# Attention as two sequences over a whole layer, outputs three tiles behind the logits, and the last product of the weights on VectorE

## The reference

```python
for l in range(DEPTH):                       # DEPTH = 2
    h = rms_norm_2(x, mix_norm_g[l])
    sb_q, sb_k, sb_v, sw_q, sw_k, sw_v, gate_logits = split(h @ w_in[l])
    y_sb = stick_breaking_attention(sb_q, sb_k, sb_v) @ w_branch_sb[l]      # 8 heads of 64
    q = rope(rms_norm_2(sw_q, q_norm_g[l])); k = rope(rms_norm_2(sw_k, k_norm_g[l]))
    y_swa = sliding_window_sink_attention(q, k, sw_v, sinks[l]) @ w_branch_swa[l]
    gates = sigmoid(gate_logits)
    x = x + (gates[0] * y_sb + gates[1] * y_swa) @ w_out[l]
    x = x + square(relu(rms_norm_2(x, mlp_norm_g[l]) @ w_up[l])) @ w_down[l]
```

## Time and profile before

| | |
|---|---|
| median of the runs | 2786.04 us |
| profiled execution, its span | 2787.14 us, 2785.7 us |
| TensorE (PE) busy | 2710.9 us, 97% |
| weight loads (PEld) | 2188.9 us |
| VectorE (DVE) busy | 1533.3 us, 55% |
| ScalarE (ACT) busy | 1173.1 us, 42% |
| GpSimd (POOL) busy | 166.7 us, 6% |
| chain that ended last | PE 84%, ACT 7%, DVE 6%, issue 2%, POOL 1% |

### The profile page before, as it was taken

How to read it: one execution, slowest core, us unless ns; L and a number is a source line. 1 busy time by engine, 2 the same in 40 slices (tenths; PEclk the granted TensorE clock), 3 DMA queues, 4 the chain that set the end, 5 groups by cost and what they waited for, 6 DMA issues and landing times.

```text
span 2785.7 us, 31002 instructions
## 1 busy us (share of the span) xinstructions
PE 2710.9 (97%) x12494; PEld 2188.9 (79%) x12494; DVE 1533.3 (55%) x2063; ACT 1173.1 (42%) x1702; POOL 166.7 (6%) x143
## 2 busy tenths in 40 slices
PE   8999999999999999999999999999999999999998
PEld 6888878888887888886666888888866668888887
DVE  4666657465687747476445554443554545544443
ACT  6444344243475424254545333332444553333322
POOL 2333110000010000000110000000001000000000
PEclk9999999999999999999999999999999999999999
DMA  4111113323333332332111232223221112222322
GB/s 170 53 57 57 52 59 106 98 89 101 106 99 103 98 98 99 99 106 76 46 38 46 91 98 92 97 98 99 98 68 39 46 46 99 91 98 94 99 95 76
DMA packets 66670, 235.55 MB, mean 85 GB/s; under 512 B 7520, under 2 KB 8032, under 8 KB 66528
## 3 DMA queue, kind: packets, MB, share of 16 engines
q1 hardware_dynamic: 63504, 228.58, 24.9%
q10 hardware_dynamic: 3024, 4.99, 0.6%
HBM read 231.44 MB, written 2.10 MB: 84 GB/s over the span
## 4 chain that ended last, share of the span: by engine, by line
PE 84%; ACT 7%; DVE 6%; issue 2%; POOL 1%; DMA 0%; SPq 0%; ACTq 0%; DVEq 0%
PE bank L411 25%; PE bank L413 25%; PE bank L412 25%; ACT w_hi_k L892 1%; DVE w_lo_k L1393 1%; PE bank L762 1%; PE bank L822 1%; ACT p_t_att L1300 1%; PE bank L801 1%; ACT L899 1%; DVE st_att L1862 1%; PE bank L753 1%; PE bank L814 1%; POOL q_mix L2000 1%; PE bank L746 0%
## 5 line engine op out<-in xcount | busy, mean ns | idle before, releaser
L411 PE MATMUL bank<-x_hi_k,w_hi_k 128*128 128x512 f32 x2152 | 868.4, 404 | 11.8 <-DVE x_lo_k L1400 10.8
L892 ACT ACTIVATE w_hi_k<-raw_k 128x1024 fp32r<-128x1024 f32 x431 | 454.5, 1058 | 937.7 <-PE bank L413 936.3
L413 PE MATMUL bank<-x_hi_k,w_lo_k 128*128 128x512 f32 x2152 | 842.9, 392 | 0.0
L412 PE MATMUL bank<-x_lo_k,w_hi_k 128*128 128x512 f32 x2152 | 842.7, 392 | 0.0
L1393 DVE TENSOR_TENSOR w_lo_k<-raw_k,w_hi_k 128x1024 fp32r<-128x1024 f32 x431 | 532.7, 1236 | 179.0 <-ACT w_hi_k L892 179.0
L411 PEld LDWEIGHTS bank<-x_hi_k,w_hi_k 128*128 128x128 f32 x2152 | 407.7, 189 | 107.9 <-issue 15.1
L413 PEld LDWEIGHTS bank<-x_hi_k,w_lo_k 128*128 128x128 f32 x2152 | 406.5, 189 | 87.3
L412 PEld LDWEIGHTS bank<-x_lo_k,w_hi_k 128*128 128x128 f32 x2152 | 407.3, 189 | 82.2 <-issue 4.1
L411 PE MATMUL bank<-y_hi_k,w_hi_k 128*128 128x512 f32 x1136 | 445.5, 392 | 3.2 <-DVE y_lo_k L1726 1.9
L413 PE MATMUL bank<-y_hi_k,w_lo_k 128*128 128x512 f32 x1136 | 442.9, 390 | 0.0
L412 PE MATMUL bank<-y_lo_k,w_hi_k 128*128 128x512 f32 x1136 | 442.7, 390 | 0.0
(11 more groups left out here) (315 smaller groups left out, 2544.2 us busy)
## 6 DMA issues: line engine op xcount, KB each, us to landing
raw_k<-wstream SPq DMA_DIRECT2D x431, 512.0 KB, 3.3
outT<-h_k ACTq DMA_DIRECT2D x8, 256.0 KB, 2.9
h_k<-xT SPq DMA_DIRECT2D x4, 256.0 KB, 8.3
h_k<-xT ACTq DMA_DIRECT2D x4, 256.0 KB, 7.7
decay_mix<-constants ACTq DMA_DIRECT2D x4, 256.0 KB, 2.6
levels_mix<-constants SPq DMA_DIRECT2D x1, 448.0 KB, 11.0
vec_k<-vectors SPq DMA_DIRECT2D x1, 282.5 KB, 9.6
cos_mix<-constants SPq DMA_DIRECT2D x1, 256.0 KB, 10.2
```

The lines of the kernel that those rows point to most:

```text
L411: pe.matmul(dst, wh, rh, start=start, stop=False)
L412: pe.matmul(dst, wh, rl, start=False, stop=False)
L413: return pe.matmul(dst, wl, rh, start=False, stop=stop)
L892: act.activation(k.w_hi[:, u % SPLIT, :], k.raw[:, u % RAW, :], ACT.Copy).then_inc(*hi_done.mark())
```

## The change

Both attention layers change alike.
- `stick` and `window` are now generators over a whole layer. `stick` counts 32 tiles through; a tile has three slots: the output of tile g - 3 (and, at a pair's start, the turned values of it), the turning of tile g - 2, the logits of tile g. `window` is a table of slots in which each pair's steps stand at fixed offsets, 24 slots from pair to pair; the halves begin at slots 10 and 22 of a pair. 105 slots of `stick`, 106 of `window` and 84 portions (21 units) of filling are woven evenly.
- The product `stick_w` x `kept` moves from GpSimd to VectorE, right behind the scan (L1833).
- The order of units: pair 0 has three units ahead of the sequence; its window queries are the first unit beside it.
- The window's queries are no longer scaled by their root mean square ahead of the rotation. The sum of squares becomes four products with two columns (L797, bank 3), the root is taken on 128 x 8 (`rq`), and goes into the exponential as its scale and into the maxima by one more small product (L1886). The rotation of the window's keys moves into the sequence as well.
- ScalarE loads the exponential's table two slots after a half's scores, and the sigmoids' right after the exponentials, in both halves.

```diff
-FIRST_PAIR = (3, 0, 1, 2)
...
+PAIRS = 4
+
+
+def beside_pairs(layer):
+
+    units = [("pair", layer, 0, 3)]
+    units += [("pair", layer, pair, n) for pair in (1, 2) for n in range(4)]
+    units += [("merge", layer, 0, 0)]
+    units += [("pair", layer, 3, n) for n in range(4)]
+    return units + [("merge", layer, m, gate) for m in range(KEPT_GATES) for gate in range(2)][1:]
...
+STICK_LAG = 3
+STICK_SLOTS = 3 * (ALL_TILES + STICK_LAG)
+PAIR_SLOTS = 3 * TILES
+HALF_AT = (10, 22)
...
-            (filling(fill, len(fill.units) * PARTS), len(fill.units) * PARTS, 0.1, 1))
+def layer_tasks(stick, window, fill):
+    return ((stick, STICK_SLOTS, 0, STICK_SLOTS / WINDOW_SLOTS), (window, WINDOW_SLOTS, 0, 1),
+            (filling(fill, len(fill.units) * PARTS), len(fill.units) * PARTS, 0, 1))
+
+
+def window_slots():
+
+    for t in range(WINDOW_SLOTS):
+        yield [(m, t - PAIR_SLOTS * m) for m in range(PAIRS)]
...
+    def stick(layer):
...
+        def logits(g):
+            half, i = STICK_ORDER[g % TILES]
+            if g % TILES == 0:
+                pe.wait_ge(*dve_done.at("qk", layer, g // TILES))
+            if g >= 2:
+                pe.wait_ge(*act_done.at("stick_keep", layer, g - 2))
...
+        for g in range(ALL_TILES + STICK_LAG):
+            if g >= 3:
+                output(g - 3)
+            if g >= 2 and (g - 2) % TILES == 0 and g - 2 < ALL_TILES:
+                values((g - 2) // TILES)
             yield
-            if n >= 2:
-                output(n - 2, *STICK_ORDER[n - 2])
-            if 1 <= n <= 2 * TC:
-                turned(n - 1, STICK_ORDER[n - 1][1])
+            if 2 <= g < ALL_TILES + 2:
+                turned(g - 2)
             yield
-        yield
...
+        def exps(m, half):
+            act.wait_ge(*dve_done.at("max", layer, m, half))
+            for n in range(TC):
+                act.activation(k.p_t[:, n, :], score_view(k, n), ACT.Exp, scale=k.rq[:, n, half:half + 1],
+                               bias=k.st[:, 1, n:n + 1], accum_out=k.st[:, 2, n:n + 1]).then_inc(*mark())
+            act.activation(k.st[:, 3, :], k.st[:, 1, :], ACT.Exp,
...
+        for slot in window_slots():
+            for m, at in slot:
+                if at == HALF_AT[0] - 3:
+                    squares(m)
+                for half in range(2):
+                    if at == HALF_AT[half] + 2:
+                        ln_exp_tables()
+                        if half == 0:
+                            act.wait_ge(*pe_done.at("wq_sum", layer, m))
+                            inverse_root(k.rq[:], wq_sums(k), 1.0 / 64, "wq_root", layer, m)
+                    if at == HALF_AT[half] + 3:
+                        exps(m, half)
+                        sigmoid_tables()
+                    if at == HALF_AT[half] + 7:
+                        act.wait_ge(*pe_done.at("pT", layer, m, half))
...
+    def stick(layer):
+        for g in range(ALL_TILES + STICK_LAG):
+            if 1 <= g <= ALL_TILES:
+                n = (g - 1) % 2
+                seen = seen_keys(STICK_ORDER[(g - 1) % TILES][1])
+                dve.wait_ge(*act_done.at("stick_keep", layer, g - 1))
+                dve.tensor_tensor_scan(k.kept[:, n, T - seen:T][:, ::-1], k.keep[:, n, 0:seen][:, ::-1],
+                                       k.zeros[:, 0:1].to_broadcast([P, seen]), 1.0, ALU.mult,
+                                       ALU.add).then_inc(*mark())
+                w = k.stick_w[:, n, 0:seen]
+                dve.wait_ge(*now())
+                dve.tensor_tensor(w, w, k.kept[:, n, T - seen + 1:T + 1], ALU.mult).then_inc(*mark("stick_w", layer, g - 1))
+                if g % TILES == 0 and g < ALL_TILES:
+                    queries_and_keys(layer, g // TILES)
             yield
...
+        def queries(m):
+            dve.wait_ge(*now())
+            dve.tensor_scalar(k.wq[:], k.lands[3][:], vcol("q_gain2", layer), None, ALU.mult).then_inc(*mark())
+            yield from rope(k.wq, k.rot, "wq", layer, m)
...
+        def offsets(m, half):
             dve.wait_ge(*now())
-            dve.tensor_scalar(k.st[:, 1, :], k.st[:, 0, :], sink, -1.0, ALU.max,
-                              ALU.mult).then_inc(*mark("max", *at, half))
-            yield
-            yield
-            dve.wait_ge(*act_done.at("exps", *at, half))
+            dve.tensor_tensor(k.st[:, 0, :], k.st[:, 0, :], k.rq[:, :, half], ALU.mult).then_inc(*mark())
+            dve.wait_ge(*now())
+            dve.tensor_scalar(k.st[:, 1, :], k.st[:, 0, :], vcol("sinks2", layer * 8 + m + half * 4), -1.0, ALU.max,
...
+        for slot in window_slots():
+            for m, at in slot:
+                if at == HALF_AT[0] - 4:
+                    turning = queries(m)
+                for half in range(2):
+                    if at == HALF_AT[half] + 1:
+                        dve.wait_ge(*pe_done.at("scores", layer, m, half))
+                        maxima(half)
+                    if at == HALF_AT[half] + (1 if half else 3):
+                        if half == 0:
+                            dve.wait_ge(*act_done.at("wq_root", layer, m))
+                        offsets(m, half)
+                    if at == HALF_AT[half] + 5:
+                        probabilities(m, half)
+                if at == HALF_AT[1] + 11:
+                    dve.wait_ge(*act_done.at("att_y", layer, m + 4))
+                    dve.tensor_tensor(k.y_lo[:, m + 4, :], k.wo[:], k.y_hi[:, m + 4, :].bitcast(F32),
+                                      ALU.subtract).then_inc(*mark("att_y", layer, m + 4))
+            next(turning, None)
             yield
...
-    for layer in range(LAYERS2):
-        for pair in range(4):
-            for n, (half, i) in enumerate(STICK_ORDER):
-                w = k.stick_w[:, n % 2, 0:seen_keys(i)]
-                pool.wait_ge(*dve_done.at("kept", layer, pair, n))
-                pool.tensor_tensor(w, w, k.kept[:, n % 2, T - seen_keys(i) + 1:T + 1],
-                                   ALU.mult).then_inc(*mark("stick_w", layer, pair, n))
```

More of the change, by code:

```diff
@@ L302, in attention_memory @@
     k.p_t, k.pT = take("p_t", [P, TC, 2 * P]), take("pT", [P, TC, 2 * P])
[L303 removed]
+    k.st, k.rq = take("st", [P, 5, TC]), take("rq", [P, TC, 2])
     arena.at = shared
@@ L769, in stick @@
             yield
[L770 to L773 removed]
+            if 2 <= g < ALL_TILES + 2:
+                turned(g - 2)
             yield
[L775 to L788 removed]
+            if g < ALL_TILES:
+                logits(g)
@@ L830, in attention @@
              between=(lambda: sum_squares(bank[7][:], k.ssum, stage)) if layer == 1 else final_sums)
-        first = Fill([("pair", layer, 0, n) for n in FIRST_PAIR], fill_piece)
+        first = Fill([("pair", layer, 0, n) for n in range(3)], fill_piece)
         first.part(4)
@@ L841, in attention @@
         first.rest()
-        for pair in range(4):
-            interleave(*pair_tasks(stick(layer, pair), window(layer, pair), Fill(between_pairs(layer, pair), fill_piece)))
+        interleave(*layer_tasks(stick(layer), window(layer), Fill(beside_pairs(layer), fill_piece)))
     def merge(layer):
@@ L1335, in attention @@
         inverse_root(k.rstd[:], bank[6][:], 1.0 / 64, "wk_root", layer)
-        window_squares(layer, 0)
         first.rest()
-        for pair in range(4):
-            interleave(*pair_tasks(stick(layer, pair), window(layer, pair), Fill(between_pairs(layer, pair), fill_piece)))
+        interleave(*layer_tasks(stick(layer), window(layer), Fill(beside_pairs(layer), fill_piece)))
     def merge(layer):
@@ L1903, in fill_piece @@
             w_low()
-        first = Fill([("kv", layer, n) for n in range(2)] + [("pair", layer, 0, n) for n in FIRST_PAIR], fill_piece)
+        first = Fill([("kv", layer, n) for n in range(2)] + [("pair", layer, 0, n) for n in range(3)], fill_piece)
         first.part(8)
@@ L1908, in attention @@
             h_final(range(KT))
-        first.part(4)
-        dve.wait_ge(*act_done.at("wk_root", layer))
-        dve.wait_ge(*now())
-        dve.scalar_tensor_tensor(k.wk[:], k.wk[:], vcol("k_gain2", layer), k.rstd[:], ALU.mult,
-                                 ALU.mult).then_inc(*mark())
-        first.part(4)
-        rope(k.wk, k.rot).then_inc(*mark())
-        dve.wait_ge(*now())
-        for half in range(2):
-            r, other = head_rows(half)
-            mm = dve.tensor_scalar(k.zwk[r, half, :], k.wk[r, :], 0.125, None, ALU.mult)
-            mm.then_inc(*(mark("wk", layer) if half else mark()))
+        first.part(8)
+        queries_and_keys(layer, 0)
         first.rest()
-        for pair in range(4):
-            interleave(*pair_tasks(stick(layer, pair), window(layer, pair), Fill(between_pairs(layer, pair), fill_piece)))
+        interleave(*layer_tasks(stick(layer), window(layer), Fill(beside_pairs(layer), fill_piece)))
     def merge(layer):
```

325 lines of the change are left out of this document (134 added, 191 removed).

## The result

| | before | changed |
|---|---|---|
| median (7 runs each) | 2786.4 us | 2794.7 us (2789.6 to 2798.5) |
| ratio | | 1.0031, 95% interval 1.0021 to 1.0041 |
| profiled execution, its span | 2787.14, 2785.7 us | 2797.0, 2795.5 us |
| TensorE busy, mean granted clock | 2710.9 us, 0.993 | 2719.0 us, 0.989 |

The change makes the kernel 8.3 us slower. The forecast was 2782 us, 4 us faster: wrong in its direction. The time lies inside the range, between the forecast and the case in which the clock falls at middling waits too (2802). Most of the effects and their sizes came out; the price of the clock did not.

The account below looks back on a forecast made before the run. TensorE, busy 97% of the span, was taken to bound the kernel. 63 us taken away against 65 added, less about 6 (59), gave -4 us: 2782 us; own range 2771 to 2793, whole range 2750 to 2806.

Parts of the forecast that it names:

- the case in which the clock falls at middling waits too: Rival: clock also falls after six TensorE waits of 2.15, 2.6 and 2.75 us, giving 2802 us; chance 0.23.
- The step that failed: Low TensorE clock behind six new waits of 4.0 to 4.2 us for the window's probabilities, charged 14 us.
- the discount: About 6 us off the added 65, for long waits sparing the clock and weight splits sometimes coming earlier.
- the wait put at 2.75 us: TensorE's wait for the window's probabilities in the second of a layer's eight halves, worked out at 2.75 us.
- What was taken away: Attention's 60 us of TensorE standstill and low clock, plus 3 us from the window's squares: together 63 us.
- all new waits gone: Extreme of the rival with probabilities nearly in time (chance 0.27, 2754 us): no new TensorE waits left, 2726 us.
- What was added: Waits for the window's probabilities 42 us, breaks 3, two smaller terms 6, low clock 14: 65 us.
- The rotated queries of the first pair: TensorE's wait for VectorE to rotate the first pair's window queries after the keys: 1.7 us, twice.
- The squares: Window's sum of squares on TensorE as four two-column products of 0.4 us: gain 3 us, ends 0 and 6.
- The breaks: TensorE's filling cut into 80 runs of products a layer instead of 65, about 0.1 us per break: 3 us.
- The rule weighed: Skill's further 1380 ns drain after ScalarE table loads, 17 us more over 12 chains, near 2799 us; not adopted.
- The pair starts: Rival: query and key copies hold back new pairs' first logits by 4 us, six times; 2820 us, chance 0.05.

Follow-up runs that it names:

- the filled runs: Changed kernel with thrown-away products ahead of the probabilities' wait: at ten places 2778.2 us, at the four middling waits only 2787.6, at the six long ones only 2776.2.
- one number in one engine's table: Changed kernel with VectorE scaling the window's probabilities at slot +4 of a half, not +5, ahead of the wide scan: 2737.6 us.
- long waits filled: Changed kernel with ten thrown-away products ahead of only the six waits of about 4 us for the probabilities: 2776.2 us.
- the kernel before, filled: Kernel before with nine thrown-away products ahead of each of the six long waits at the starts of pairs 1, 2 and 3: 2784.1 us.
- one slot later: Changed kernel with the turning of the probabilities, ScalarE's copy of them and the window half's output one slot later (+8, +10): 2747.7 us.
- product back on GpSimd: Changed kernel with the product of the stick weights on GpSimd again, only the scan on VectorE: 2790.6 us.

## Why the prediction was wrong

- **The step that failed is the clock's.** It charged 14 us for the six waits of about 4 us and took 6 off, because not each would bring the clock down and the split of weights might come earlier. All six did (16.2 us by the windows), the four of 2.16 and 2.68 us did as well (6.7), and one at the rotated queries (1.7). So 24.6 us stood where 8 were written. From wait to wait, as the filled runs showed, the ten falls at L822 cost some 21 of their 22.9. The prediction's own sign for this rival, low clock after more than eight waits, came: it was eleven. The prediction knew that nothing in the trace lay between 1.7 and 3.94 us and made the fall there a rival with 0.23; the discount had no row at all. Without the discount the forecast is 2788, and with the rival's 14 us 2802. The measured 2794.7 lies between them, since the middling falls cost 1.6 us each at four places, not 2.4 at six (2788 + 6.4 = 2794): the wait put at 2.75 us came as two, 1.42 at L822 and 1.30 at the output L776, and the clock fell behind neither. That this sum meets the time so closely is partly luck, for the other misses named below cancel: 3 us of gain that did not come and 1.7 of a fall at the rotated queries, against 3 us for the outputs' low parts and 2.9 of small waits.
- **What was taken away: right.** The 60 us of standstill and low clock left the trace, save 2.6 us at the stick outputs. The low clock of the kernel before, worth only 3 us by itself there, could count in full here, because the waits for the rotated queries of pairs 1 to 3 that it covered went too. With nearly all of the new wait gone too, 2737.6 us were measured; the prediction's case "all new waits gone" said 2726, and the 2737.6 still holds 9.6 us of idle time.
- **What was added: right in its sum.** 42 us at L822 against 39.9 plus 16 times 0.16, and half by half save the second, which came in two parts. The rotated queries of the first pair: 1.7 forecast, 1.93 measured. The low part of a finished output was to cost 0.5 us three times a layer and cost nothing.
- **The squares: wrong.** Four small products with two columns each (eight instructions) were put at 0.4 us. In the changed kernel they take 0.91 up to the next product, as the rows below show; the nearest rows had 0.89 for what went. A gain of 3 us was none.
- **The breaks: right.** The rows below show one: the first filling product behind it starts 0.32 us ahead of its neighbour, where 0.23 is the rule. With some 15 more breaks in each layer that makes about 2.6 us, against 3 forecast.

```profile
1303.86 1.05 PE L797 MATMUL bank<-con_k,sq_k 128*128 128x2 f32 x8
1304.77 0.48 PE L424 MATMUL bank<-x_hi_k,w_hi_k 128*128 128x512 f32 x1
1305.09 0.40 PE L425 MATMUL bank<-x_lo_k,w_hi_k 128*128 128x512 f32 x1
1305.32 0.40 PE L426 MATMUL bank<-x_hi_k,w_lo_k 128*128 128x512 f32 x1
```
- **Small waits.** L736 (1.6 us, gone) and L814 (1.3 us, the old wait for the probabilities, now part of L822's) were left at nothing. Taken off as well, they are 2.9 us.
- **The rule weighed.** The next activation starts 1.30 us behind the load's start in the changed kernel too; the further 1380 ns that the Trainium skill (ScalarE: Activation LUTs, "What ACT_TABLE_LOAD costs") states are in no row, and the sum without them met seven of a layer's eight waits to some 0.3 us. That its 2799 us lie nearer to the measured time than the forecast does has another cause, the clock.
- **The own range.** An error of 0.6 us on each of 14 waits is 8.4 us, so 2774 to 2790, not the 2771 to 2793 that were written.
- **The pair starts** wait nowhere; that rival is out.

## What to carry to other kernels

Ask of every moved step what now stands ahead of the instruction that the bounding engine waits for: here one number in one engine's table was worth 57 us, twenty times what the product's move brought. Price low clock by what would be waited for without it: it can be cover (14 us worth 3 in the kernel before) or come on top of a wait. A discount on a measured cost needs a row of its own; where the trace has a gap, give the forecast the middle, not the kind end.

## What the runs showed of the hardware

- Length of one wait does not decide whether the clock falls. It fell behind 1.86 (long waits filled), 1.90 (the kernel before, filled), 1.93, 2.16 and 2.68 us, and stayed up behind 2.23 and 2.40 (one slot later), 2.14 (long waits filled), 2.51 (product back on GpSimd) and 3.08 us until a second wait of 2.46 followed. One place behaves differently in two executions or two layers: the wait of 1.93 us at L808 in the changed kernel has 1.00 behind it in the first layer and 0.79 in the second. What decides it these runs leave open.
- Added work whose result is thrown away can make a kernel faster: the changed kernel with 76 products more is 16.5 us quicker. In the kernel before, 108 of them brought 3 us.
- A four-part scaling on VectorE that starts 0.22 us into a product on GpSimd takes 1.80 us in place of 1.14, and its first part ends 0.14 us behind the product, in twelve of twelve places.
- Products with two columns take 0.11 us each (eight in 0.91 us), half of what 512 columns take.
